# First loads of a hybrid trunk step: token rows lead SP's queue, filter loads and decay rates go through ScalarE's, decay factors are computed, two adaLN quarters stand among the transposes

## What is computed

```python
def trunk_layer(x, mods, p, ctx_k, ctx_v):
    shift1, scale1, gate1, shift2, scale2, gate2 = mods      # silu(cond) @ w_ada + b_ada
    h = modulate(rms_norm(x, p['g_pre_mix']), shift1, scale1)
    m, k, v = parallel_mixer(h, p, ctx_k, ctx_v)             # attention beside a hyena long convolution
    ...
def hyena_filter(L, f1_w, f1_b, sin_freq, f2_w, f2_b, f3_w):
    t = jnp.linspace(0.0, 1.0, L)
    z = jnp.concatenate([t[:, None], jnp.cos(ang), -jnp.sin(ang)], axis=-1)
    h = jnp.sin(freq * (z @ f1_w + f1_b))
    h = jnp.sin(freq * (h @ f2_w + f2_b))
    h = h @ f3_w
    deltas = jnp.abs(jnp.linspace(min_decay, max_decay, HY_WIDTH))
    decay = jnp.exp(-t[:, None] * deltas[None, :])
    h_fwd = h[:, :HY_WIDTH] * decay
    h_bwd = h[:, HY_WIDTH:] * decay
```

## Time and profile before

| what | value |
|---|---|
| median of 3 runs | 2291.67 us (2289.37 to 2293.55) |
| profiled execution | span 2289.1 us, first to last instruction; the views give no other time for it |
| TensorE products busy | 95% |
| VectorE, ScalarE, GpSimd busy | 47%, 16%, 6% |
| transfers, mean over the span | 283 GB/s |

### The profile page before, as it was taken

One profiled execution on the slowest core, in us unless ns is written; L12 is line 12 of the kernel. 1 busy time (PEld: TensorE's weight loads), 2 busy tenths in 40 slices (PEclk: granted clock), 3 DMA queues, 4 the chain that ended last, 5 costly groups with the idle time before them and its releaser, 6 DMA issues.

```text
span 2289.1 us, 26778 instructions
## 1 busy us (share of the span) xinstructions
PE 2173.7 (95%) x10755; PEld 1373.2 (60%) x10755; DVE 1078.6 (47%) x1701; ACT 370.7 (16%) x937; POOL 137.5 (6%) x143
## 2 busy tenths in 40 slices
PE   6999999999999999999999999999998888989997
PEld 3389974467899999999986853333332222222223
DVE  6198998776777678766654331100111110102114
ACT  3011110012443441100000221010110000000002
POOL 0001100013111110000000001100000000000000
PEclk9999999999999999999999999999999999999999
DMA  9954553342442334443463569999999999999997
GB/s 393 427 223 187 209 200 143 152 191 81 191 178 114 145 148 190 179 184 148 184 248 124 195 256 396 402 413 428 421 428 420 427 429 427 424 429 427 426 422 311
DMA packets 54293, 647.71 MB, mean 283 GB/s; under 512 B 6150, under 2 KB 6696, under 8 KB 9128
## 3 DMA queue, kind: packets, MB, share of 16 engines
q1 hardware_dynamic: 51992, 637.66, 67.8%
q10 hardware_dynamic: 2192, 8.52, 0.9%
HBM read 642.47 MB, written 3.69 MB: 282 GB/s over the span
## 4 chain that ended last, share of the span: by engine, by line
PE 74%; DMA 19%; DVE 3%; issue 1%; DVEq 1%; ACT 1%; ACTq 0%; POOL 0%; SPq 0%; POOLq 0%
PE PS L898 28%; DMA ring<-in_w_gate_up 15%; PE PS L1548 8%; PE PS L1587 7%; PE PS L756 5%; PE PS L1376 4%; PE PS L1075 3%; PE PS L1361 2%; DMA ring<-in_w_down 2%; PE PS L1509 2%; PE PS L1062 2%; PE PS L745 1%; PE PS L1663 1%; PE PS L1628 1%; DMA ring<-in_w_ada 1%
## 5 line engine op out<-in xcount | busy, mean ns | idle before, releaser
L1548 PE MATMUL PS<-ring,RF 128*48 128x512 f32 x1568 | 357.8, 596 | 49.5 <-DMA ring<-in_w_gate_up 47.8
L2431 DVE SCALAR_TENSOR_TENSOR RG<-ring,SM,RG 128x512 f32<-128x512 f32 x450 | 329.0, 769 | 17.4 <-issue 1.3
L1548 PEld LDWEIGHTS PS<-ring,RF 128*48 128x48 f32 x1568 | 97.3, 123 | 295.9 <-issue 192.9
L898 PE MATMUL PS<-RB,ring 128*128 128x192 f32 x1376 | 233.3, 327 | 0.6 <-ACT RE L1803 0.6
L898 PEld LDWEIGHTS PS<-RB,ring 128*128 128x128 f32 x1376 | 224.9, 190 | 6.8 <-ACT RE L1803 1.9
L3294 DVE TENSOR_TENSOR RB<-RB,PS 128x512 f32<-128x512 f32 x84 | 56.6, 685 | 360.2 <-PE PS L1509 360.1
L1587 PE MATMUL PS<-ring,RF 128*48 128x512 f32 x832 | 189.5, 613 | 5.3 <-DMA ring<-in_w_down 3.0
L3299 DVE TENSOR_TENSOR RG<-RF,PS 48x512 f32<-48x512 f32 x32 | 22.1, 690 | 300.9 <-ACT RF L2101 268.3
L1587 PEld LDWEIGHTS PS<-ring,RF 128*48 128x48 f32 x832 | 56.0, 127 | 136.0 <-issue 127.7
L898 PE MATMUL PS<-RE,ring 128*128 128x192 f32 x768 | 130.1, 326 | 0.0
L756 PE MATMUL PS<-ring,RB 128*128 128x512 f32 x288 | 126.9, 593 | 0.0
(11 more groups left out here) (468 smaller groups left out, 2889.3 us busy)
## 6 DMA issues: line engine op xcount, KB each, us to landing
ring<-in_w_gate_up SPq DMA_DIRECT2D x104, 2048.0 KB, 14.6
ring<-in_w_ada SPq DMA_DIRECT2D x48, 2048.0 KB, 8.7
ring<-in_w_down SPq DMA_DIRECT2D x44, 2048.0 KB, 15.7
ring<-in_w_in SPq DMA_DIRECT2D x38, 2048.0 KB, 7.9
ring<-in_w_gate_up SPq DMA_DIRECT2D x28, 1024.0 KB, 9.0
ring<-in_w_attn_o SPq DMA_DIRECT2D x8, 2048.0 KB, 7.5
ring<-in_w_out SPq DMA_DIRECT2D x8, 2048.0 KB, 7.7
ring<-in_w_down SPq DMA_DIRECT2D x16, 1024.0 KB, 9.8
```

The lines of the kernel that those rows point to most:

```text
L898: last = mm(bank(b, TH), w(k), x(k), start=start and k == 0, stop=k == kn - 1, skip_group_check=not start)
L1548: last = mm(bank(n, p0=64 * u, p1=64 * u + SLOTS), xeT[:, 0, kk, :] if first else x_cur[:, kk, :], homes[home_of(at, 2 * i + u)][:, k * FF ...
L2431: last = stt(out=acc[c], in0=w, scalar=cond[:, kk, c:c + 1], in1=acc[c], op0=ALU.mult, op1=ALU.add)
```

## The change

The token rows become SP's first loads. The four loads of the filter's inputs move to the front of ScalarE's program, with a new one between them: the 1024 decay rates, broadcast to 128 partitions (0.5 MB), in place of the 1.5 MB table. `fv` gets three more columns with the negative times, and ScalarE makes `dec` by three exponentials of 128x1024 ahead of the first sine. The first square stands behind the first sine instead of ahead of it, and the two Silus ahead of the scaling of the prompt rows. Quarters 0 and 1 are used behind the transposes of groups 3 and 7 instead of behind all of them. The banks of the transposes change from 4, 5, 7 to 4, 6, 0, since quarters occupy 5 and 7; group 2 so waits for the first tap product to be read.

```diff
@@ sync
-            sp.dma_start(zf[0:HE, :], zfeat).then_inc(filt_in, 16)
-            sp.dma_start(f1[0:HE, :], f1_w).then_inc(filt_in, 16)
-            sp.dma_start(f2[0:HF, :], f2_w).then_inc(filt_in, 16)
-            sp.dma_start(fv, f_vec).then_inc(filt_in, 16)
             sp.dma_start(xn[:, 0, :], x_prompt).then_inc(x_in, 16)
             for m in range(1, MT):
                 sp.dma_start(xn[:, m, :], x_sample[(m - 1) * P:m * P, :]).then_inc(xs_in[m - 1], 16)
             sp.dma_start(f3, f3_w).then_inc(f3_in, 16)
-            sp.dma_start(dec[:, 0, :], decay[0]).then_inc(dec_in, 16)
-            sp.dma_start(dec[:, 1:3, :], decay[1:3].rearrange("m p d -> p m d")).then_inc(dec_in, 16)
@@ tensor
+            pe.wait_ge(cond_ready, 2)
             for k in range(KT):
+                if k == 2:
+                    pe.wait_ge(f_taps, 1)
...
                 last.then_inc(tr1, 1)
+                if k in (3, 7):
+                    ada_quarter(0, k // 4)
...
-            for j in range(4):
+            for j in range(2, 4):
                 ada_quarter(0, j)
@@ scalar
+            act.dma_start(fv, f_vec).then_inc(filt_in, 16)
+            act.dma_start(rates, decay.to_broadcast([P, HYW])).then_inc(rates_in, 16)
+            act.dma_start(zf[0:HE, :], zfeat).then_inc(filt_in, 16)
+            act.dma_start(f1[0:HE, :], f1_w).then_inc(filt_in, 16)
+            act.dma_start(f2[0:HF, :], f2_w).then_inc(filt_in, 16)
             act.dma_start(col, cols).then_inc(small_in, 16)
             act.dma_start(KC[:, N_COLS:N_COLS + N_TABS], tabs).then_inc(small_in, 16)
...
+            act.wait_ge(filt_in, 64)
+            act.wait_ge(rates_in, 16)
+            for m in range(MT):
+                A(dec[:, m, :], rates, ACT.Exp, scale=fv[:, 3 + m:4 + m]).then_inc(dec_ready, 1)
+            act.wait_ge(f_arg, 1)
+            A(arg, arg, ACT.Sin).then_inc(f_sin, 1)
             act.wait_ge(x_in, 16)
             squares(0)
-            act.wait_ge(f_arg, 1)
-            A(arg, arg, ACT.Sin).then_inc(f_sin, 1)
...
-            act.wait_ge(roots, 1)
-            A(xn[:, 0, :], xn[:, 0, :], ACT.Copy, scale=rstd[:, 0:1]).then_inc(xn1_a, 1)
             act.wait_ge(small_in, 32)
             act.wait_ge(cond_ready, 1)
...
+            act.wait_ge(roots, 1)
+            A(xn[:, 0, :], xn[:, 0, :], ACT.Copy, scale=rstd[:, 0:1]).then_inc(xn1_a, 1)
@@ vector
-            dve.wait_ge(dec_in, 32)
+            dve.wait_ge(dec_ready, MT)
```

More of the change, by code:

```diff
@@ L150, in build @@
         zf = view(RE, 11264, T)
-        fv = view(RE, 11776, 3)
+        fv = view(RE, 11776, 6)
+        rates = view(RA, 0, HYW)
         hyT = view(RE, 0, 3 * HYT, T)
@@ L238, in build @@
         HY_B, H0, H1, B_Q0, B_Q, B_S, B_P, B_O = ((4, 5), (2, 3)), (3, 5), (4, 2), 5, 6, (0, 1), (0, 1), 6
-        B_T, B_TR1 = (0, 1, 6, 7), (4, 5, 7)
+        B_T, B_TR1 = (0, 1, 6, 7), (4, 6, 0)
         B_DOWN = ((2, 3), (0, 1), (2, 3), (0, 1))
@@ L263, in build @@
         piece_used, gu_done, down_done = sem("piece_used"), sem("gu_done"), sem("down_done")
-        small_in, x_in, filt_in, f3_in, dec_in, dft_in, inv_in, qk_in, cache_in, xres_in, wr_in = (
-            sem(n) for n in ("small_in", "x_in", "filt_in", "f3_in", "dec_in", "dft_in", "inv_in", "qk_in",
+        small_in, x_in, filt_in, f3_in, rates_in, dec_ready, dft_in, inv_in, qk_in, cache_in, xres_in, wr_in = (
+            sem(n) for n in ("small_in", "x_in", "filt_in", "f3_in", "rates_in", "dec_ready", "dft_in", "inv_in", "qk_in",
                              "cache_in", "xres_in", "wr_in"))
@@ L828, in latent_spectrum @@
                 last.then_inc(f_dft, 1)
-            pe.wait_ge(cond_ready, 2)
             pe.wait_ge(tr1_v, KT // 2)
@@ L3428, in positions @@
         z = np.concatenate([t[:, None], np.cos(ang), -np.sin(ang)], axis=-1).astype(f32)
[L3429 to L3434, removed]
+        return z, t
+    zc, tc = positions(TC)
+    zl, tl = (v[np.concatenate([2 * p, 2 * p + 1])] for v in positions(TL))
     zfeat = np.ascontiguousarray(np.concatenate([zc, zl]).T)
-    decay = np.concatenate([dc, dl]).reshape(MT, P, HYW)
+    times = np.ascontiguousarray(-np.concatenate([tc, tl]).reshape(MT, P).T)
+    decay = np.abs(np.linspace(math.log(1e-2) / 1.5, math.log(1e-2) / 0.3, HYW, dtype=f32)).reshape(1, HYW)
     half = HD // 2
@@ L3446, in tables @@
     rope = np.ascontiguousarray(rope.transpose(1, 0, 2, 3)).astype(f32)
-    return tabs, dft_all, zfeat, decay, rope
+    return tabs, dft_all, zfeat, times, decay, rope
 def quarter_tiles(w):
@@ L3496 @@
         columns(a["hy_conv_w"]), columns(a["hy_conv_b"]), columns(a["hy_skip"])], axis=1))
-    f_vec = np.tile(np.concatenate([a["hy_f1_b"], a["hy_sin_freq"], a["hy_f2_b"]]).T, (2, 1))
     f3_w = np.concatenate([a["hy_f3_w"][0][:, :HYW], a["hy_f3_w"][0][:, HYW:]])
-    tabs, dft, zfeat, decay, rope = tables()
+    tabs, dft, zfeat, times, decay, rope = tables()
+    f_vec = np.concatenate([np.tile(np.concatenate([a["hy_f1_b"], a["hy_sin_freq"], a["hy_f2_b"]]).T, (2, 1)), times], axis=1)
     router = np.zeros((P, KT, 32), np.float32)
```

## The result

The changed kernel takes 2297.09 us (median of 13 runs, 2294.58 to 2298.79) against 2291.67 before (13 runs too): a ratio of 1.0023, 95% interval 1.0015 to 1.0030, so 5.4 us slower. I had said 2294.1, with a range up to 2298.0. The sign of the sum was right and its size was not: +2.4 us foretold, +5.4 measured. The profiled execution of the changed kernel has a span of 2296.1 us, 7.0 longer than the one before; it was itself one of the longer ones (2297.88 us, where the median is 2297.09).

What follows compares the result with a forecast made beforehand. Full transfers and TensorE, two chains nearly side by side into 107.3 us, were taken to bound. Filter loads at 11.0 put the last transpose at 39.0; less 36.6 gives +2.4 on 2291.67, so 2294.1 us, range 2288.3 to 2298.0.

Steps and rivals of the forecast that it cites:

- One packet for one: First loads: SP's and ScalarE's queues alternate packet for packet, so each small filter packet waits for one 8 KB token packet (0.31 us).
- rival 1: First loads: the filter loads aren't held up and land at 4.8 to 8 us; time 2290, at best 2287.9; chance 0.20.
- rival 2: First loads: SP gets over one turn per ScalarE turn; slower from landing at 13.2, two for one 14.6, 2297.7 us; chance 0.17.
- B = 11.0: Start: the four filter loads have landed at 11.0 us instead of 4.29, after 18 packets per engine taking turns with SP's.
- main case: First loads: queues alternate one for one, filter loads land at 9 to 13 us, taken as 11.0; +2.4 us; chance 0.58.
- main sum: Start to about 107 us: filter loads landed at 11.0, last transpose at 39.0, so the end is 2.4 us later.
- T = B + 28.0: Filter path: the last of 48 transposes comes 28.0 us after the filter loads land, at 39.0, two quarters among the transposes.
- T to the end: Last transpose to last adaLN block: shift is its moment less 36.6 through TensorE or less 37.1 through transfers; the later binds.
- The saving lost in a hole: Transfers: first loads end 5 us sooner, 1.05 MB fewer moved, but engines idle from about 33 to 40 us.
- The shift reaches the end: Behind 107.3 us every load follows a release by another engine, so the +2.4 us there reaches the end undiminished.
- Rival 3: First loads: transfers alone decide and the whole 4.6 us is saved, 2287.1 us; SP goes on by 33.4; chance 0.02.

Runs made afterwards that it cites:

- a3: The changed kernel with one more 3 KB load (128 rows of 24 bytes) on ScalarE's queue, which the filter path awaits: 2298.26 us, ratio 1.0038.
- b3: The kernel before with decay factors made on the chip and ScalarE's first work reordered, filter loads first on SP's queue, quarters behind the taps: 2291.28 us, ratio 1.0003.
- a1: The changed kernel with its four filter loads back at the head of SP's queue: 2290.75 us against 2291.30 before, ratio 0.9995.
- b4: The kernel before with quarters 0 and 1 among the transposes and the fifth adaLN block issued ahead of SP's wait for the transposes: 2290.11 us, ratio 0.9994.
- a4: The changed kernel with filter loads back on SP's queue and the fifth adaLN block issued ahead of SP's wait for the transposes: 2286.60 us, ratio 0.9982.
- b1: The kernel before with only the filter loads moved to ScalarE's queue and the token rows first on SP's: 2295.33 us, ratio 1.0018.
- a2: The changed kernel with quarters 0 and 1 back behind the tap products: 2300.02 us against 2291.07 before, ratio 1.0039.
- b2: The kernel before with only quarters 0 and 1 moved among the transposes, with the banks and waits this needs: 2291.39 us, ratio 0.9999.
- a6: The changed kernel with only the fifth adaLN block issued ahead of SP's wait for the transposes, filter loads left on ScalarE's queue: 2294.93 us, ratio 1.0020.
- a5: The changed kernel with filter loads on SP's queue, fifth adaLN block issued early, and quarter 0 alone among the transposes: 2286.89 us, ratio 0.9981.

## Why the prediction was right in sign and half in size

- *One packet for one.* Right, and exactly so (50 and 50, 51 and 51). Neither rival holds: the small loads don't slip through (rival 1), and SP gets no second turn (rival 2). The Trainium skill (DMA: Bandwidth & Descriptors, Queues, rings and completion order) has an engine drain a whole packet, typically of some 9 to 17 descriptors, from one queue before it switches. If a descriptor is what the profile counts as a packet, this trace does not agree: from 3 to 14 us the counts of the two queues are within four of each other in every microsecond, with 29 to 90 packets each.
- *B = 11.0.* The step that failed. Measured 13.77. I counted 18 turns from 3.2 us on and let the 128 rows of `f_vec` pass free, as if they were through by then. They were not: they took turns from 2.9 to 5.35 us, and the first 4 KB row of the rates moved at 5.4, not at 3.2. With them it is 26 turns; the eight missing ones at 0.31 are 2.5 us of the 2.8, and the closing packet that each load has on each engine (a3) makes it nine, 2.8. With B over 13.2 the result came out where rival 2 had its threshold, but by the mechanism of the main case. That the measured time still lies in the range is luck: the range reached to 2298.0 only to make room for rival 2, which did not happen. Rival 2's own number was off as well: by the terms of the main sum, two turns for one give B = 11.0 + 5.5 = 16.5 and not 14.6.
- *T = B + 28.0.* 28.7 measured. Transposes at B+16.8 (16.9 foretold), the fourth group at B+19.6 (19.7), exponentials 3.23 us (3.2) and hidden. The two quarters and the other transposes took 9.2 us instead of 8.35: the quarters 1.87 each (33.82 to 35.69, 37.37 to 39.24) where a fourth of 7.10 is 1.78, and the transposes around them 5.4, where 5.2 less the 0.4 that the copies should give back is 4.8. So the 0.4 was a term that didn't come.
- *T to the end.* Of the two chains the other one bound. TensorE's came out at T - 37.2 (6.95 less the 1.6 of waits that are left, with T = 42.5), 0.6 below the T - 36.6 foretold. For the transfers I said T - 37.1, and it was T - 35.6: from SP's issue to the use of the last block 71.7 us instead of 70.2. The bytes were right, but a block has landed only when the slowest engine is through with it: from 38.7 us to 107 the kernel before moved 28.8 MB on SP's queue (2233 packets), where the loads up to that block are 28.3, so up to 0.5 MB, 1.2 us, belonged to later loads. In the changed kernel it was 29.2 MB from 42.54 to 114.27, 0.9 MB more than the loads up to that block. That is how I read it; no run tries it.
- *The saving lost in a hole.* Right: empty from 34 to 42 us, and b3 and a1 show that the saved megabyte buys nothing while SP is held. b4 and a4 show by their traces that it does once the hole is closed.
- *The shift reaches the end.* Right in the profiles: 6.95 us at 129, 7.4 at 950, 7.0 in the span. Between the medians it is 5.4. Of the 1.6 that are missing, 0.8 is that the profiled execution was longer than the median of its kernel; the rest stays open. Foretold were 2.4 us at 107, so by the traces the shift was nearly three times as large as I had it.
- *Rival 3* (transfers alone, a full gain of 4.6 us) asked for B under 5.4 and SP going on by 33.4. By its own sum (T - 37.1) it needed T = 32.5 and B = 4.5. a4 has B = 5.87 with SP going on at 27.95, and gains 4.5 us, so a gain was there to be had and the release withheld it. That 4.5 is so near to 4.6 proves nothing: in a4 TensorE binds and not the transfers, and its hyena products start only 2.8 us sooner.

By the runs, the parts of the change are: filter loads on the second queue +4 us alone; the decay factors made on the chip 0, since their rates load delays the small loads by 1.9 us and SP is held anyway; the quarters among the transposes 0 alone, and some 3.5 us saved where the filter loads are late. They don't add up one by one: with the rates load in among the small loads B is another 3.7 us later (9.96 in b1, 13.62 in a2), which is how a2 comes to +9, and the quarters take back some 3.5 of that.

## What to carry to other kernels

In these traces two queues of one core alternate packet for packet, so a small load's price beside a bulk load is its number of packets per engine times the time of one of the other queue's packets, whatever its bytes: small loads that start a chain belong ahead of the bulk on the bulk's queue, or should be few packets. A megabyte less to move is worth nothing while the issuing engine is held at a release; look for the hole first, and ask of each wait in the list which of the loads behind it needs it. And when adding up turns, count the packets of every load in the queue, those of the smallest too.

## What the hardware did that I had not expected

TensorE's granted clock falls to its lower level for some 3 us now and then, at different places in different executions of nearly the same program. Here it does in b1, where TensorE had waited for a block at 111 (columns as above, the clock is the third from the end; 1.00 is 2.4 GHz, 0.50 is 1.2):

```profile
111.00:112.00 1.00, 0.07 (x4) 0.07 (x8) 0.00 (x0) 0.00 (x0) 0.00 (x0) 0.78 1.02 426
112.00:113.00 1.00, 1.00 (x8) 0.33 (x12) 0.00 (x0) 0.00 (x0) 0.00 (x0) 0.50 1.07 451
113.00:114.00 1.00, 1.00 (x10) 0.20 (x4) 0.00 (x0) 0.00 (x0) 0.00 (x0) 0.50 1.04 442
```

The block's products took 3.41 us there instead of 1.92, so b1's profile is 1.5 us later behind it than its loads explain. b4 has such a fall from 107 to 110, again behind a wait for a block (2.9 us), b2 one from 25 to 29, among the transposes, a2 two, at 33 to 37 and 108 to 112. The kernel before has a wait of the same length, 3.0 us, and no fall behind it, so the wait alone doesn't bring it on, and what does stays open.

From 1386 us on every profile has several more, in part at different places. This is where a3's 3.1 us went. The rows of before and then of a3:

```profile
1300.00:1400.00 100.00, 95.53 (x520) 53.06 (x520) 32.36 (x81) 23.64 (x45) 5.15 (x6) 0.98 0.78 297
1400.00:1500.00 100.00, 98.31 (x429) 34.88 (x427) 15.25 (x29) 7.47 (x13) 10.42 (x6) 0.98 0.98 398
```

```profile
1300.00:1400.00 100.00, 95.53 (x528) 58.47 (x528) 35.09 (x83) 24.41 (x47) 3.35 (x5) 1.00 0.73 277
1400.00:1500.00 100.00, 98.30 (x435) 35.50 (x433) 15.15 (x29) 7.47 (x13) 12.23 (x7) 1.00 1.00 411
```

Before has two falls there, a3 none; the five profiles with one (b1, b4, a2, a4, a6) lose 1.4 to 1.5 us of shift in this stretch, those with two (b2, b3, a5, changed) nothing, and a1, with three, gains 1.5. So two single profiles can differ by 1.5 us for each such fall for no reason in the program, and differences of that size should be read from medians.
